# Products of the identity in the waits of the attention stages

## The reference

```
# first block, layer 0 and layer 1
y = concat([moba(q, k, v) * silu(g), fox(q, k, v, cumsum(log f)) * silu(g)])
x = x + y @ w_out_ab
oc = (softmax(q1 k1) - lam * softmax(q2 k2)) @ v      # diff: 4 heads of 2 maps
y = concat([rmsnorm(oc) * silu(g), swa(q, k, v, sinks) * silu(g)])
x = x + y @ w_out_cd
# second block, i = 0, 1
h = h + (mla_mixer if i == 0 else stick_breaking_mixer)(rmsnorm(h))
h = h + mem_cross_attn(rmsnorm(h), rmsnorm(mem))      # xa: 4 heads
h = h + square(relu(rmsnorm(h) @ w_in)) @ w_out
```

## Time and profile before

| | us |
|---|---|
| median of three runs | 1068.36 |
| the profiled execution, whole | 1072.39 |
| its span, first to last instruction | 1070.6 |
| PE busy in it | 1001.8 |
| DVE busy | 637.2 |
| ACT busy | 544.5 |
| mean granted clock of PE, of 2.4 GHz | 0.967 |

### The profile page before, as it was taken

How to read it: one execution, slowest core, us unless ns; L and a number is a source line. 1 busy time by engine, 2 the same in 40 slices (tenths; PEclk the granted TensorE clock), 3 DMA queues, 4 the chain that set the end, 5 groups by cost and what they waited for, 6 DMA issues and landing times.

```text
span 1070.6 us, 15661 instructions
## 1 busy us (share of the span) xinstructions
PE 1001.8 (94%) x6152; PEld 889.3 (83%) x6152; DVE 637.2 (60%) x1202; ACT 544.5 (51%) x1015; POOL 42.4 (4%) x80
## 2 busy tenths in 40 slices
PE   6998899999798988997999999999999989999996
PEld 5877778786686878986899999899988869999995
DVE  4867855484855465745775555556873657654552
ACT  5466564464565344635654444454673456444351
POOL 2110400000111000000000000000000000000000
PEclk9999899999888999999999999999999989999998
DMA  7966313554322334442366555656435415555650
GB/s 244 256 122 156 109 50 112 165 172 143 116 82 69 75 98 115 157 135 102 120 196 193 176 184 195 236 159 191 148 102 188 157 45 193 185 182 186 196 177 39
DMA packets 117685, 158.61 MB, mean 148 GB/s; under 512 B 17814, under 2 KB 59116, under 8 KB 117612
## 3 DMA queue, kind: packets, MB, share of 16 engines
q1 hardware_dynamic: 117612, 157.61, 47.9%
HBM read 156.55 MB, written 1.05 MB: 147 GB/s over the span
## 4 chain that ended last, share of the span: by engine, by line
PE 81%; DVE 7%; ACT 5%; issue 3%; DMA 2%; SPq 1%; POOL 1%; DVEq 0%; POOLq 0%; ACTq 0%
PE bank L464 24%; PE bank L465 23%; PE bank L466 23%; PE bank L596 2%; DMA raw<-in_w_in_ab 2%; DVE w_lo L1581 2%; PE bank L621 2%; PE bank L610 2%; PE bank L518 2%; ACT pb L1289 1%; ACT w_hi L1160 1%; SPq L2210 1%; PE bank L630 0%; DVE nl L1763 0%; PE bank L581 0%
## 5 line engine op out<-in xcount | busy, mean ns | idle before, releaser
L1581 DVE TENSOR_TENSOR w_lo<-raw,w_hi 128x1024 fp32r<-128x1024 f32 (+3 forms) x300 | 343.4, 1190 | 194.4 <-ACT w_hi L1160 194.0
L1160 ACT CAST w_hi<-raw 128x1024 fp32r<-128x1024 f32 (+3 forms) x300 | 289.9, 1025 | 158.9 <-DMA raw<-in_mlp_w_in 73.9
L464 PE MATMUL bank<-xT_hi,w_hi 128*128 128x256 f32 x792 | 226.2, 286 | 2.7 <-DVE xT_lo L1631 1.8
L466 PE MATMUL bank<-xT_hi,w_lo 128*128 128x256 f32 x792 | 224.3, 283 | 0.0
L465 PE MATMUL bank<-xT_lo,w_hi 128*128 128x256 f32 x792 | 224.3, 283 | 0.0
L464 PE MATMUL bank<-w_hi,xT_hi 128*128 128x512 f32 (+1 forms) x432 | 165.0, 382 | 6.0 <-DVE w_lo L1581 3.7
L465 PE MATMUL bank<-w_lo,xT_hi 128*128 128x512 f32 (+1 forms) x432 | 161.0, 373 | 0.0
L466 PE MATMUL bank<-w_hi,xT_lo 128*128 128x512 f32 (+1 forms) x432 | 160.6, 372 | 0.0
L464 PEld LDWEIGHTS bank<-xT_hi,w_hi 128*128 128x128 f32 x792 | 152.2, 192 | 4.4 <-issue 2.6
L465 PEld LDWEIGHTS bank<-xT_lo,w_hi 128*128 128x128 f32 x792 | 152.2, 192 | 0.6
L466 PEld LDWEIGHTS bank<-xT_hi,w_lo 128*128 128x128 f32 x792 | 152.1, 192 | 0.0
(11 more groups left out here) (218 smaller groups left out, 1085.0 us busy)
## 6 DMA issues: line engine op xcount, KB each, us to landing
raw<-in_mlp_w_in SPq DMA_DIRECT2D x32, 1024.0 KB, 5.3
raw<-in_mlp_w_out SPq DMA_DIRECT2D x32, 1024.0 KB, 5.1
raw<-in_w_in_ab SPq DMA_DIRECT2D x16, 1024.0 KB, 11.4
raw<-in_w_in_cd SPq DMA_DIRECT2D x13, 1024.0 KB, 5.1
raw<-in_xa_w_kv SPq DMA_DIRECT2D x8, 1024.0 KB, 4.9
raw<-in_sb_w_qkv SPq DMA_DIRECT2D x16, 512.0 KB, 5.1
raw<-in_w_out_ab SPq DMA_DIRECT2D x4, 1024.0 KB, 5.1
raw<-in_w_out_cd SPq DMA_DIRECT2D x4, 1024.0 KB, 5.1
```

The lines of the kernel that those rows point to most:

```text
L464: pe.matmul(o, wh, ih, start=start, stop=False, skip_group_check=True)
L466: return pe.matmul(o, wl, ih, start=False, stop=stop, skip_group_check=True)
L1160: nc.scalar.copy(w_hi[:, u % SLOTS, a], raw[:, u % SLOTS, a]).then_inc(hi_ready, 1)
L1581: V.tensor_tensor(w_lo[:, u % SLOTS, a], raw[:, u % SLOTS, a], w_hi[:, u % SLOTS, a].bitcast(F32), ALU.subtract).then_inc(lo_ready, 1)
```

## The change

`busy(b, n)` writes n products of the identity with itself into bank b. It is called right behind `begin` for the bank and ahead of the wait for the data: in `turn_probs` by the table BUSY_TURN, in `values` and `deep` by BUSY_VALUES, in `mla_head(0)` (8) and ahead of the first MLA scores (7). In all 82 products: moba head 4: 7; fox head 1: 6; diff, transposes of heads 0 to 3: 5, 7, 4, 8, values of heads 0 and 3: 2 and 3; swa, values of head 3: 6, transposes of heads 5 to 7: 2, 2, 3; MLA 8 and 7; the values of head 0 of both cross attentions: 6 each. In `deep`, `begin` for the values is called ahead of `busy`, and `values_T` skips its own.

```diff
+            def busy(b, n):
+
+                for _ in range(n):
+                    pe.matmul(banks[b][:, 0:P], ident[:, :], ident[:, :], start=True, stop=True)
+
+            BUSY_TURN = {("diff", 0): 5, ("diff", 1): 7, ("diff", 2): 4, ("diff", 3): 8, ("swa", 5): 2, ("swa", 6): 2, ("swa", 7): 3}
+            BUSY_VALUES = {("moba", 4): 7, ("fox", 1): 6, ("swa", 3): 6, ("diff", 0): 2, ("diff", 3): 3, ("xa", 0): 6}
+
             def turn_probs(k):
                 g = k["g"]
                 begin(("PT", g), 6)
+                busy(6, BUSY_TURN.get((k["kind"], k["h"]), 0))
...
                 begin(("Y", g), 7)
+                busy(7, BUSY_VALUES.get((k["kind"], k["h"]), 0))
                 pe.wait_ge(probsT_ready, k["turn"])
...
                 begin(("q", h), b)
+                if h == 0:
+                    busy(b, 8)
...
                     if i < len(ks):
+                        if i == 0 and ks[0]["kind"] == "mla":
+                            b = 4 + ks[0]["g"] % 2
+                            begin(("S", ks[0]["g"]), b)
+                            busy(b, 7)
                         ready(i)
                         scores(ks[i])
                     if 3 <= i:
                         k = ks[i - 3]
+                        begin(("Y", k["g"]), 7)
+                        busy(7, BUSY_VALUES.get((k["kind"], k["h"]), 0))
                         pe.wait_ge(probsT_ready, k["turn"])
-                        values_T(k, ("Y", k["g"]), k["pt"], k["v"], full=k["kind"] == "xa")
+                        values_T(k, ("Y", k["g"]), k["pt"], k["v"], full=k["kind"] == "xa", begun=True)
```

More of the change, by code:

```diff
@@ L623, in values, with values_T @@
                 end(("Y", g), ins, (y_ready, k["output"]))
-            def values_T(k, name, pt, v, full=False):
-                begin(name, 7)
+            def values_T(k, name, pt, v, full=False, begun=False):
+                if not begun:
+                    begin(name, 7)
                 o = banks[7][:, 0:S]
```

## The result

| | before | changed |
|---|---|---|
| median, 15 runs each | 1069.69 (1064.68 to 1074.40) | 1075.61 (1073.28 to 1078.15) |
| ratio, 95% interval | | 1.0042 [1.0023, 1.0061] |
| profiled execution, whole | 1072.39 | 1076.53 |
| mean granted clock in it | 0.967 | 0.982 |

The change makes the kernel 0.42% slower by the ratio, about 4.5 us; the two medians alone differ by 5.9 us. A second comparison, with 12 runs of it and 28 of before, gave 1.0069 [1.0038, 1.0100], 7.4 us. The forecast was 1066.9 us, which is 1.5 us (0.14%) under the three runs of before that it had and 0.26% under the median above. The measured 1075.61 us lies above its range (1062 to 1072.8). It was wrong.

A forecast was written before the change was run, and what follows sets the result against it. PE was taken to set the end almost everywhere, slowed by half-clock stretches; +9.5 us path cost less 12.1 us clock gain gave -2.6, -0.4 with the gain scaled, and -1.5 between them: 1066.9 us, range 1062 to 1072.8.

The forecast's parts named there:

- Which products are paid: All 82 products: 43 on PE's path, behind bank or weight waits or without cover, are paid; 39 are covered.
- The view of a stage that DVE ends: Diff stage: DVE ends PE's waits, so the low-clock stretches at 259.31 and 269.55 are not worth much.
- The price of 0.22: Each of the 43 path products costs 0.22 us even at half clock: +9.5 us, upper bound +17.2.
- the third of the stretch at 293.44: Diff 3: the 10.24 us half-clock stretch could end sooner; a third of its 4.1 us loss, 1.4, counted as gain.
- The gain of 12.1: Clock regained at MLA scores, both cross attentions and swa tail (10.7 us) plus 1.4 at 293.44; range 0 to 22.6.
- The scaling by 0.82: Whole kernel: a median run loses 18.6 of 22.6 us to low clock, so the gain is 9.9, total -0.4.
- The sum: Whole kernel, profiled execution: 9.5 us path cost less 12.1 us clock gain, -2.6 us against 1072.39.
- the forecast of -1.5: Whole kernel: value taken between -2.6 and -0.4 us, giving 1066.9 us; chance 0.43.
- Rival 1: Bank-wait work is paid and the clock not kept; under 8 us of loss goes away: about +4, 1072 us; chance 0.27.
- Rival 2: Denser work behind the waits holds the clock too (stretches at 120, 150, 293, 331, 396): 1063.6 us; chance 0.17.
- Rival 3: The diff stage is on the path after all; stretches at 259.31 and 269.55 return 4.9 us more: 1062; chance 0.08.
- rival 4: Identity products don't hold the clock, so nothing comes back: +9.5, 1077.9 us; chance 0.05.

The follow-up runs named there:

- e2: The changed kernel with only the 43 products behind bank or weight waits or on the path, against before: ratio 1.0091 [1.0058, 1.0124], +9.7 us.
- e1: The changed kernel with only the 39 products inside data waits, against before: ratio 0.9976 [0.9952, 1.0000], -2.6 us.
- e4: The e2 kernel with each group three times as long (129 products), against before: ratio 1.0268 [1.0238, 1.0299]; 18.5 us slower than e2.
- e14: The changed kernel, nothing altered, profiled a third time: 34.1 us at half clock, partly in other places than in its other three profiles.
- e12: The kernel before, nothing altered, profiled a third time: ends at 1064.90 us, with 47.8 us at half clock.
- e16: The kernel before with 82 identity products added behind PE's last instruction: 51 instruction packets, three transfers in 13.6 us, 3.06 us late at 102 us.
- e8: The kernel before with only the 20 early products inside waits (diff heads 0 to 2, swa 5): ratio 1.0013 [0.9993, 1.0032].
- e7: The kernel before with only the 19 later products inside waits (MLA scores, both cross attentions): ratio 0.9967 [0.9940, 0.9994].

## Why the prediction was wrong

**Which products are paid: right.** All five groups read from the earlier trace rows start behind their wait, which is as long as before to 0.33 us except at diff 3 (2.64 for 3.79), and e2 and e1 have opposite signs. The filled waits shrank: 2.02 to 0.81 at diff 0, 2.72 to 1.05 at the MLA scores, 2.59 to 1.83 in the cross attention. At diff 1 the 2.90 us stay as they are: PE, without the stretch at 259, comes to this wait 1.6 us sooner than before, measured from the wait of diff 0, and the seven products fill just that. DVE releases it 11.5 us after that of diff 0, as before. The view of a stage that DVE ends held.

**The price of 0.22: right for a product, too low for the groups.** At the full clock a product costs 0.225 (mla head 0), and 0.19 to 0.215 in e4. I had reasoned that a stretch at half clock ends at a given time, so that added work costs what it does at full rate, and put the other reading (it grows with the work) only at the upper end. The stretches behind fox 1 and swa 3 have 3.41 us in three of before's four profiles, and 6.83 in three of the changed kernel's. For moba 4 to mla head 0, with the values of diff 3 and the third of the stretch at 293.44, 1.5 + 1.3 + 0.4 + 2.0 + 1.8 = 7.0 us had been forecast; the table has 2.3 + 3.6 + 2.0 + 3.1 + 2.1 = 13.1, of which 0.8 comes back by 281.9. Of these 5.3, 1.6 lie at diff 3, where the third of the stretch did not come back. Most of the rest fits the two stretches that grew. From 129.9 to 170 us, around fox 1, PE is busy at half clock for 6.6 us on average of the changed kernel's four profiles and 4.0 of before's; half of the difference is 1.3 of the 1.7 too many there. From 306 to 330 us, at swa 3, it is 2.0 against none, and half of it is 1.0 of the 1.1 too many. The stretch at moba 4 has kept its length but in e14; the 0.8 us too many there are idle time. In all four changed profiles the wait ahead of the products is 3.30 to 3.33 us, before 2.64 to 3.29, and behind them PE waits again for DVE, which only one of before's four does:

```profile
136.30 1.55 PE L596 MATMUL bank<-arena 64*128 64x128 f32 x8 [0.54 <-DVE arena L1935]
```

So the reason given for 0.22 throughout, that a stretch at half clock ends at a given time, held at moba 4 and not at fox 1 and swa 3. Where a stretch came to lie on a group that it had missed before, the products cost twice as much, as at mla head 0 in e14.

**The gain of 12.1: nearly right.** The MLA scores and cross attentions gave 6.2 where 7.6 stood, and the swa tail -2.8 with its products' cost where -2.0 stood. The stretch behind mla head 0, which I had left standing, went as well in three of four (1.2); e1, which has no products there, and one profile of before (e12) lack it too, so no run shows that the products did it. Not won was the third of the stretch at 293.44, which two of before's four profiles don't have.

**The scaling by 0.82: right in its reason, wrong in its size.** Executions of before do differ in their half clock (47.8 to 68.3 us), and the profiled one was on the long side. But the medians of the later sets of runs of before were 1069.7 to 1071.6, so the 4.0 us between it and the first three runs lay mostly in those three.

**What failed is a term that the sum did not have.** Between 80 and 118 us 4.7 of the final 7.2 us are lost. The sum began at the first added instruction and took all ahead of it as unchanged, without giving a reason. Without that step the changed kernel would be 7.2 - 4.7 = 2.5 us later, or 7.2 - 3.6 = 3.6 if only as much of it reaches the end as in e16 (estimates both): still slower, mostly by the grown stretches, so the forecast of -1.5 would have missed by 4 even then. The whole account, for the profiled execution: the sum was -2.6 and the mean of the profiles is +7.2. Of the 9.8 between them (to rounding) 4.5 stand at 118 us, 5.3 come from the groups behind their waits, 1.4 are missing at the MLA scores and cross attentions and 0.7 are lost behind the second one; the swa tail gave 0.8 and the stretch behind mla head 0 1.2 more than forecast.

**The rivals.** Rival 1 has the number (+4) and not the way: it needed under 8 us of loss to go away, and the gains of the table are 2.8 + 1.2 + 1.4 + 1.1 + 3.7 = 10.2, the first of them with its products' cost of 1.1 already taken off. Its first half, that the work behind the waits is paid, is what e2 shows. Rival 2 (denser work behind the waits holds the clock) isn't borne out by the changed kernel: the stretch at moba 4 stayed, and those at fox 1 and swa 3 were longer in three of four profiles. With three times the work (e4) it is true in part, 0.16 to 0.215 us for a product instead of 0.22. Rival 3 falls with e8, rival 4 with e7 and with every stretch that went. The total at half clock was forecast as 27 us and is 34.1: 6.83 of it is the one at 86.18, behind the late transfer.

The prediction weighed two ways to price a stretch: half of its length wherever it lies, or half of PE's busy time and only on the path. The two stretches of the diff stage are gone in three of the changed kernel's profiles and next to no time came back (0.1 us from 250 to 282.6 us; e8 1.0013), so a stretch off the path isn't worth half its length, as the earlier trace rows said. The median clock of the runs rose from 0.970 to 0.982, which over 1072 us is 12.9 us less lost, while the time grew: PE's clock is a poor measure of such a change.

## What to carry to other kernels

Work meant to fill a wait must stand ahead of the semaphore that ends it last: read the releaser of each wait from the timeline first, since 43 products on the wrong side of it cost 0.9%, and a set with 35 of them moved ahead of it gained 0.6 to 0.9%. Where an effect is under 1%, profile each kernel several times and compare the starts of the same instructions by stage; one pair of profiles would have given any of several stories. And look at the stretch ahead of the first changed instruction: adding instructions anywhere can move it.

## What the runs showed of the hardware that I had not expected

- The length of the program changes how long early weight transfers take: 9.4, 9.8 and 13.6 us for the same three 128 KB transfers with 49, 50 and 51 packets on the queue of instructions, and 3 us at 102 us in e16_at_end, which adds its instructions at the very end.
- The same kernel in different executions spends 47.8 to 68.3 us at half clock, and runs of before spread from 1063.3 to 1079.0 us. Over 28 of them time and mean clock go together: 1063.7 to 1064.9 at 0.975, 1076.1 to 1079.0 at 0.963 to 0.966.
- Products of the identity with itself can hold the clock: 6 of them, with 1.82 us of idle time left behind, were enough. The stretch of 10.24 us behind the second cross attention is in none of the ten profiles that have them and in eight of the nine that don't; the ninth is e4. So products aren't the only thing that decides whether a stretch comes, and nothing tried here shows what else does.
